# Five projection chunks of a decoder trunk from feature layout to token layout, with queries ahead of lx

## The reference

```python
(r_q, r_k, r_v, a_cq, a_ckv, a_kpe, l_x, l_v, l_o, l_i, l_f, c_q, z) = _split_cols(x @ w_in, IN_SPLITS)
ret  = ...retention(r_q, r_k, r_v)
mla  = ...latent attention(a_cq, a_ckv, a_kpe)
xc   = silu(_causal_conv(l_x, ml_conv_w, ml_conv_b))          # lx: conv over time, 4 taps
mls  = ...mLSTM(xc, l_v, l_i, l_f) * sigmoid(l_o)... + ml_skip * xc
k, v = split(mem @ w_mem_kv)                                  # memory keys and values, 256 memory tokens
memo = softmax(heads(c_q) @ k.T * d ** -0.5) @ v              # memory cross-attention, 4 heads of 128
y    = concat([ret, mla, mls, memo]) * silu(z)                # z: 4 x 512 gates
x    = LayerNorm(ALPHA * x + y @ w_out)
```

## Time and profile before

| | us |
|---|---|
| median of 3 runs | 901.63 (901.59 to 901.67) |
| the profiled execution's own time | 902.31 |
| its span | 900.5 |

### The profile page before, as it was taken

How to read it: one execution, slowest core, us unless ns; L and a number is a source line. 1 busy time by engine, 2 the same in 40 slices (tenths; PEclk the granted TensorE clock), 3 DMA queues, 4 the chain that set the end, 5 groups by cost and what they waited for, 6 DMA issues and landing times.

```text
span 900.5 us, 13869 instructions
## 1 busy us (share of the span) xinstructions
PE 893.0 (99%) x4836; PEld 776.0 (86%) x4836; DVE 659.0 (73%) x1308; ACT 490.5 (54%) x926; POOL 16.0 (2%) x18
## 2 busy tenths in 40 slices
...
GB/s 358 280 318 162 148 160 234 187 141 216 240 231 253 214 211 213 194 194 198 189 188 143 307 223 159 171 252 163 154 256 166 282 180 163 234 199 230 339 98 94
DMA packets 62452, 187.75 MB, mean 208 GB/s; under 512 B 7336, under 2 KB 15792, under 8 KB 61744
## 3 DMA queue, kind: packets, MB, share of 16 engines
...
q10 hardware_dynamic: 576, 1.05, 0.3%
...
HBM read 177.13 MB, written 9.71 MB: 207 GB/s over the span
## 4 chain that ended last, share of the span: by engine, by line
PE 95%; DMA 2%; issue 1%; ACT 1%; DVE 0%; SPq 0%; POOL 0%; POOLq 0%; ACTq 0%; DVEq 0%
PE acc L1319 22%; PE acc L1304 17%; PE acc L1305 17%; PE acc L1308 17%; PE acc L1325 11%; PE work L1061 1%; PE work L1060 1%; PE work L1059 1%; PE work L1054 1%; DMA B<-turn 1%; DMA B<-mrow 1%; PE work L1209 1%; PE work L1208 1%; DMA B<-in_mem_t 0%; PE work L1220 0%
## 5 line engine op out<-in xcount | busy, mean ns | idle before, releaser
L1391 DVE TENSOR_TENSOR lo<-raw,hi 128x512 fp32r<-128x512 f32 (+2 forms) x607 | 386.4, 657 | 185.2 <-ACT hi L1018 174.7
L1018 ACT ACTIVATE hi<-raw 128x512 fp32r<-128x512 f32 (+2 forms) x607 | 351.8, 603 | 279.0 <-PE acc L1308 160.0
L1304 PE MATMUL acc<-hi,xx 128*128 128x512 f32 (+2 forms) x576 | 212.5, 373 | 0.4 <-ACT hi L1018 0.4
L1305 PE MATMUL acc<-hi,xx 128*128 128x512 f32 (+2 forms) x576 | 209.0, 366 | 0.0
L1319 PE MATMUL acc<-xx,hi 128*128 128x512 f32 x768 | 193.3, 393 | 0.4 <-ACT hi L1018 0.4
L1308 PE MATMUL acc<-lo,xx 128*128 128x512 f32 (+2 forms) x576 | 163.9, 366 | 0.0
L1319 PEld LDWEIGHTS acc<-xx,hi 128*128 128x128 f32 x768 | 138.1, 189 | 25.4 <-issue 0.5
L1304 PEld LDWEIGHTS acc<-hi,xx 128*128 128x128 f32 x576 | 108.5, 188 | 17.2 <-issue 0.8
L1305 PEld LDWEIGHTS acc<-hi,xx 128*128 128x128 f32 x576 | 108.6, 189 | 16.3
L1308 PEld LDWEIGHTS acc<-lo,xx 128*128 128x128 f32 x576 | 104.3, 188 | 17.4
L1325 PEld LDWEIGHTS acc<-xx,lo 128*128 128x128 f32 x768 | 104.8, 190 | 7.5
...
## 6 DMA issues: line engine op xcount, KB each, us to landing
raw<-in_w SPq DMA_DIRECT2D x263, 512.0 KB, 3.8
...
B<-turn SPq DMA_DIRECT2D x40, 128.0 KB, 3.9
turn<-B SPq DMA_DIRECT2D x6, 512.0 KB, 5.8
...
Y<-in_x_t SPq DMA_DIRECT2D x4, 512.0 KB, 8.7
turn<-Y SPq DMA_DIRECT2D x4, 512.0 KB, 6.5
```

The source lines that it names most:

```text
L1018: act.activation(place(l, t, hi), raw[:, s, (t % 2) * w:(t % 2 + 1) * w], ACT.Copy)\
L1304: pe.matmul(o, ah[:, q], hi[:, s, 0:w], start=k == 0, stop=False, skip_group_check=name == "memv")
L1305: pe.matmul(o, al[:, q], hi[:, s, 0:w], start=False, stop=False, skip_group_check=name == "memv")
L1391: dve.tensor_tensor(place(l, t, lo), raw[:, s, (t % 2) * w:(t % 2 + 1) * w], place(l, t, hi).bitcast(F32), ALU.subtract).then_inc(lo_done. ...
```

## The change

memk, cq, z3, z2 and z1 become one 512-wide `tok` chunk of 16 slots each, where each was two feat chunks of 8 slots. cq moves ahead of lx: memk is slots 16 to 31, cq 32 to 47, lx0 and lx1 48 to 63, and z3, z2, z1 176 to 223. lx and z0 stay feat. Since tokens now lie on partitions, DVE transposes each chunk straight from PSUM (`turn`, which replaces two `part` and two `joined`), and SP does the DRAM exchange. The reads of the turned tile (memk and cq splits, silu) follow later in the stream. The eight conv steps move from slots 54 to 61 to slots 70 to 79, `silu_conv` from 65, 66 to 82, 83, the evacuation of `ml_fold` from 77 to 84, and the steps of the gates to later slots. PE's table of steps is not changed.

```diff
-CHUNKS = [("memv", W, "tok"), *_halves("memk", "lx", "cq"),
+CHUNKS = [("memv", W, "tok"), ("memk", W, "tok"), ("cq", W, "tok"), *_halves("lx"),
...
-          ("rq", W, "tok"), ("rk", W, "tok"), ("rv", W, "tok"), *_halves("z3_", "z2_", "z1_", "z0_"),
+          ("rq", W, "tok"), ("rk", W, "tok"), ("rv", W, "tok"), 
+          ("z3", W, "tok"), ("z2", W, "tok"), ("z1", W, "tok"), *_halves("z0_"),
...
-        (65, "silu_conv", 0), (66, "silu_conv", 1), (62, "cq", 0), (70, "cq", 1), (84, "akv", 0), (85, "akv", 1),
-        (77, "ml_fold", 0), (93, "ml_q", 0), (94, "ml_q", 1),
+        (50, "memk", 0), (51, "memk", 1),
+        (82, "silu_conv", 0), (83, "silu_conv", 1), (64, "cq", 0), (65, "cq", 1), (84, "akv", 0), (85, "akv", 1),
+        (84, "ml_fold", 0), (93, "ml_q", 0), (94, "ml_q", 1),
...
-    _put(DVE_AT, 54 + _j, "conv", _j)
+    _put(DVE_AT, (70, 71, 72, 73, 74, 75, 77, 79)[_j], "conv", _j)
...
+        (36, "turn", "memk"), (52, "turn", "cq"), (196, "turn", "z3"), (213, "turn", "z2"), (229, "turn", "z1"),
+        (61, "joined", "lx", 0), (69, "joined", "lx", 1), (237, "joined", "z0_", 0), (245, "joined", "z0_", 1),
...
-        (206, "y_lo", 0), (208, "y_lo", 1), (222, "y_lo", 2), (224, "y_lo", 3),
-        (244, "y_lo", 4), (245, "y_lo", 5), (251, "y_lo", 6), (252, "y_lo", 7)]:
+        (214, "y_lo", 0), (215, "y_lo", 1), (232, "y_lo", 2), (233, "y_lo", 3),
+        (248, "y_lo", 4), (249, "y_lo", 5), (251, "y_lo", 6), (253, "y_lo", 7)]:
...
+TURN_OUT_AT = {23: "memk", 30: "cq", 57: "c", 74: "rot", 77: "cell", 81: "rq", 89: "mla0", 90: "rk", 95: "mla1",
+               102: "z3", 111: "z2", 112: "ret", 119: "z1"}
+TURN_IN_AT = {26: "memk", 33: "cq", 59: "c", 76: "rot", 79: "cell", 83: "rq", 92: "mla0", 93: "rk", 98: "mla1",
+              105: "z3", 114: "z2", 116: "ret", 122: "z1"}
...
+                    if name in READ_FROM_ACC:
+                        wait_chunk(dve, l, CI[name])
...
                     dve.transpose(squares[name].rearrange("p (b k r) -> p k b r", b=4, r=32),
-                                  turn_from[name].rearrange("p (k b c) -> p k b c", b=4, c=32))\
-                       .then_inc(squared[name].sem, 1)
+                                  src.rearrange("p (k b c) -> p k b c", b=4, c=32)).then_inc(squared[name].sem, 1)
```

More of the change, by code:

```diff
@@ L181 @@
         (180, "rv", 0), (181, "rv", 1), (184, "rkT", 0), (186, "rkT", 1),
[L182 to L185, removed]
+        (208, "silu", 3, 0), (209, "silu", 3, 1), (226, "silu", 2, 0), (227, "silu", 2, 1),
+        (243, "silu", 1, 0), (243, "silu", 1, 1), (245, "silu", 0, 0), (247, "silu", 0, 1),
+        (213, "y_hi", 0), (214, "y_hi", 1), (231, "y_hi", 2), (232, "y_hi", 3),
+        (247, "y_hi", 4), (248, "y_hi", 5), (250, "y_hi", 6), (252, "y_hi", 7)]:
     _put(ACT_AT, _s, *_step)
@@ L427, in build_trunk, with turned_tokens, by_square @@
         squares["mla1"], turn_to["mla1"] = Y[:, 2048:2048 + 6 * P], B[7][:, 0:6 * P]
+        for g in (3, 2, 1):
+            squares[f"z{g}"], turn_to[f"z{g}"] = Y[:, g * 1024:(g + 1) * 1024], B[5][:, 0:1024]
+        squares["memk"], turn_to["memk"] = B[8][:, 0:1024], B[7][:, 0:1024]
+        squares["cq"], turn_to["cq"] = B[5][:, 0:1024], B[4][:, 0:1024]
+        def turned_tokens(name, i):
+            return turn_to[name].rearrange("p (a i j r) -> p i j a r", a=4, i=NT, j=4)[:, i]
+        def by_square(buf, i):
+            return buf[:, :, i * P:(i + 1) * P].rearrange("p j (a r) -> p j a r", a=4)
         def turned_head(name, h):
@@ L459, in build_trunk @@
         acc_read = [signal(f"acc_read{p}", 0, before=2) for p in range(2)]
-        joined, lo_part = signal("joined", 14), signal("lo_part", 14)
+        joined, lo_part = signal("joined", 4), signal("lo_part", 4)
         kq_split = signal("kq_split", 4)
@@ L505, in build_trunk @@
         roped = signal("roped", 4)
-        squared = {n: signal(f"squared_{n}", 2 if n[:3] in ("mem", "mla") else 1) for n in TURNS}
+        squared = {n: signal(f"squared_{n}", 2 if n in ("mla0", "mla1") else 1) for n in TURNS}
         turn_out = {n: signal(f"turn_out_{n}", 1, step=16) for n in TURNS}
@@ L586, in A @@
             return acc[:, acc_turn(l, CI[name])[1], i, :]
-        JOINED = [("memk", 0), ("memk", 1), ("lx", 0), ("lx", 1), ("cq", 0), ("cq", 1),
-                  *((f"z{g}_", q) for g in (3, 2, 1, 0) for q in range(2))]
+        JOINED = [("lx", 0), ("lx", 1), ("z0_", 0), ("z0_", 1)]
         def wait_joined(eng, l, name, q):
@@ L597, in sums @@
                 return LX[:, 2 * q:2 * q + 2, PAD:PAD + SEQ]
[L598 to L600 removed]
+            return yT[:, 2 * q:2 * q + 2, :]
         def uq_high(l):
@@ L624, in operand @@
                 h, rest = {"memk": mKT, "cq": cQT}[name]
-                return sums(name, i), h[:, 2 * i:2 * i + 2, :], rest[:, 2 * i:2 * i + 2, :], kq_split.sem
+                return turned_tokens(name, i), by_square(h, i), by_square(rest, i), kq_split.sem
             if name == "mem_pT":
@@ L693, in _ @@
                           .then_inc(mlaw_in.sem, 16)
-                    if l == 1 and m == 32:
-                        wait_chunk(sp, l, CI["memk1"])
+                    if l == 1 and m == 36:
+                        wait_chunk(sp, l, CI["memk"])
                         sp.dma_start(gb0_place[:, :], a["gb"][0:1, :].partition_broadcast(P).rearrange("p o n -> p (o n)"))\
```

65 lines of the change are left out of this document (37 added, 28 removed), and 6 rows, old and new, of tables (ACT_AT, DVE_AT).

## The result

The median is 917.66 us (4 runs, 916.62 to 920.07), where the kernel before took 901.65 us in the same session (901.59 to 901.76): a ratio of 1.0181, 95% interval 1.0161 to 1.0201. The profiled execution took 917.66 us. It is slower, as predicted, but by 16.0 us and not by 8.8; the time lies 2.2 us above the range.

The account below looks back on a forecast made before the run. PE's own matmuls were taken to bound the kernel: span 900.5 - 5.6 saved + 14.4 of waits in akv = 909.3 us, plus 1.13 to the median, so 910.4 us; own range 907.5 to 915, 8 in 10 905.5 to 915.5.

Parts of the forecast that it names:

- The bound and the gain: Whole kernel: PE's matmuls set the time, and 160 moved slots at 0.035 us save 5.6 us.
- The stretch: Conv in akv, waits from slot 77 to 87: PE loses 7.2 us in each layer, 14.4 in all.
- 1, slot 77: Slot 77: conv makes mem_max(0), its exponential and the high part late; PE waits 1.15 us.
- 2, low part of 78 and `mem_pT(0)`: Slot 78: PE waits 0.45 us for DVE's low part, then 0.45 for mem_norm(0) with mem_pT(0).
- 3, slot 81: Slot 81: its high part comes after mem_max(1) and mem_exp(1); PE waits 1.9 us.
- 4, slots 83 and 84: Slots 83 and 84: a table load and two silu steps on ACT delay high parts; 0.6 us for both.
- 5, `mem_pT(1)`: At slot 84 ACT also evacuates ml_fold, so mem_pT(1) gets its bank late; PE waits 0.65 us.
- 6, slot 87: Slot 87: its high part comes after mem_max(2) and its exponential; PE waits 2.0 us.
- Table switch twice: Rival: a table switch between exponentials costs ACT twice 1.3 us, up to 2.6 a layer, 915.6 us; chance 4%.
- two ends: Other ends of two terms taken as zero: exchange 2 us, gates pile-up 1 us, up to 3 a layer at most.
- the exchange comes late too: Rival: turned cq, asked for at slot 64, lands 5 us late, so conv starts late; 918 us, chance 6%.
- The burst of gates: Slots 243 to 253: DVE has 14.0 us of work against 10 slots of 1.36; taken as zero.

Follow-up runs that it names:

- e2: The changed kernel with identity in place of silu in silu_conv, so no table is loaded between mem_exp(1) and mem_exp(2); 915.49 us, ratio 1.0166.
- e1: The changed kernel with each of conv's sixteen operations a layer on 32 columns instead of 256; 915.43 us, ratio 1.0152.
- e3: The changed kernel with both conv on 32 columns and identity in place of silu; 911.33 us, ratio 1.0107.
- f4: The changed kernel with one operation of conv instead of sixteen in each layer; 908.58 us, ratio 1.0092.
- g3: The changed kernel with only later readers of the exchanged tiles and earlier z1 transfers; 913.83 us, ratio 1.0135.
- g2: f3 with the low parts of the memory keys at slots 62 and 63 and the load of gb back at pair 32; 898.73 us, ratio 0.9965.
- f3: The order of the kernel before, with memory keys, z3 and z2 as tok chunks and memory keys split at slots 57 to 59; 903.84 us, ratio 1.0024.

## Why the prediction was partly right

*The bound and the gain hold.* 5.6 us less was predicted, 5.7 were measured.

*The stretch was right step by step.* The table has PE's wait as predicted and as measured in layer 0 (the growth of the difference between the starts of before and after), in us:

| step | predicted | measured |
|---|---|---|
| 1, slot 77 | 1.15 | 1.71 |
| 2, low part of 78 and `mem_pT(0)` | 0.90 | 1.07 |
| 3, slot 81 | 1.9 | 1.75 |
| 4, slots 83 and 84 | 0.6 | 0.60 |
| 5, `mem_pT(1)` | 0.65 | 0.69 |
| 6, slot 87 | 2.0 | 1.84 |
| smaller pieces | 0 | 0.2 |
| in all | 7.2 | 7.86 |

Step 1 was short by 0.56. Of that 0.35 is conv: a slot with it costs DVE 1.31 us and not 1.24, since the prediction took the cheaper kind of step, 0.90, for all five. Some 0.2 more is in the start: the split of slot 71 begins 98.89 - 94.75 = 4.14 us after slot 64, where 3.95 was reckoned. "Table switch twice" fell with e2: the kernel with two loads less gained 1.4 us a layer, about the 1.28 of one row, and in the timeline above the activation follows 0.02 us behind the load; the drain that the Trainium skill adds ("ScalarE: Activation LUTs", section "What ACT_TABLE_LOAD costs") is not seen here either.

*Failed step one: "After slot 87 neither engine has anything that it did not have before", and so no loss.* True of the work, not of the lead, the time from the end of a split to PE's first matmul with it. Rows of before: the high part of slot 87 is the first of four and takes 0.47 us, and PE starts the slot at 116.72; further down are the low part of slot 99 and PE's first matmul with it.

```profile
114.91 1.66 ACT L1018 ACTIVATE hi<-raw 128x328 fp32r<-128x328 f32 x4
...
116.72 0.31 PE L1304 MATMUL acc<-hi,xx 128*128 128x328 f32 x1
...
134.15 0.67 DVE L1391 TENSOR_TENSOR lo<-raw,hi 128x512 fp32r<-128x512 f32 x1
...
135.03 0.62 PE L1308 MATMUL acc<-lo,xx 128*128 128x512 f32 x2
```

After, slot 87 again:

```profile
123.72 1.57 ACT L1030 ACTIVATE hi<-raw 128x328 fp32r<-128x328 f32 x4
...
124.24 0.42 PE L1316 MATMUL acc<-hi,xx 128*128 128x328 f32 x1 [1.65 <-ACT hi L1030]
```

So the high part of slot 87 was ready 1.34 us ahead of PE before, and 0.05 after. From `mem_exp(2)` to the gates, the softplus and the scan, DVE and ACT follow one chain, which gains nothing on PE by slot 99, where 0.21 us was to spare. The sum is 1.34 - 0.05 - 0.21 + 0.05 = 1.13, and 1.14 / 1.16 were measured. In e1, e2, e3, f4 and g3, all with 0.05 at slot 87, slots 88 to 104 took 23.73 to 23.79; in g2, with 1.36 / 1.42, 22.61 and 22.60. f3 stands between: 1.24 in layer 0, where slot 99 loses nothing, and 0.42 in layer 1, where it loses 0.85. The cost is 2.3 us in all.

*Failed step two: "In each case there are some 5 us over, so I take nothing" for the exchange.* It cost 3.8 us by g3, and up to 4.35 in one layer of e1. The two durations from the earlier trace rows were right as medians (6.2 or 6.7 out and 4.4 in, after). Missing were the places in SP's queue: outward and inward transfer stand at set pairs, with weight loads between, which wait for free buffers. The time at hand was as reckoned: 18.3 us from the start of the transposition to ACT's asking (51.7 to 69.96 in layer 0), where "14 slots" made 19. SP also waited for outward DMAs of tiles in `B` to land before it issued the inward ones, 14.6 us in six waits where it was 11.2 in four before. How much of the lateness of z2 and z1 each of these makes was not followed. The bound of 2 us a layer, kept in the range's "two ends", was right in size; it should have been the middle. The rival "the exchange comes late too" gave 918, near the outcome, but by luck. It has late queries, with conv late behind them. The queries were late for ACT, but the stretch is 22.4 us with that wait and without it (g3). What cost PE time were the memory keys, z2 and z1, each at its own place.

*The rest.* The burst of gates at slots 243 to 253 cost nothing by itself (19.06 and 19.07 in g3). A transposition from PSUM takes 1.242 us, as from SBUF (1.238), so that unknown was nil. The `gb` load at pair 36, named and taken as nothing, is hidden by the other waits in the changed kernel; in f3 it cost 1.8 us and, through the lost lead, 0.9 more.

In short: 8.8 us predicted; 1.3 more in the stretch, 2.3 at slot 99, 3.7 for late tiles (beside the rows of g3), 0.5 less at slots 104 to 112 in layer 0 (DVE's longest wait for `mrow` is 3.1 us, 3.9 before) make 15.6 on the span, where 15.4 were measured.
